# Latent attention: both query tiles' score products of a pair of heads issued together

## What is computed

```python
def mla_attend(q_nope, q_rope, k_nope, k_rope, v):
    scale = (MLA_NOPE_DIM + MLA_ROPE_DIM) ** -0.5
    s = (jnp.einsum("bqhd,bkhd->bhqk", q_nope, k_nope)
         + jnp.einsum("bqhr,bkr->bhqk", q_rope, k_rope)).astype(jnp.float32) * scale
    p = jax.nn.softmax(s, axis=-1)
    return jnp.einsum("bhqk,bkhe->bqhe", p.astype(v.dtype), v)
```

## Time and profile before

| | us |
|---|---|
| median of three runs | 3077.1 |
| lowest and highest run | 3072.35 and 3080.65 |
| the profiled execution (its span) | 3078.2 |
| busy in it: TensorE, VectorE, ScalarE, GpSimd | 3009.2, 1838.9, 1474.6, 1102.2 |

### The profile page before, as it was taken

One profiled execution on the slowest core, in us unless ns is written; L12 is line 12 of the kernel. 1 busy time (PEld: TensorE's weight loads), 2 busy tenths in 40 slices (PEclk: granted clock), 3 DMA queues, 4 the chain that ended last, 5 costly groups with the idle time before them and its releaser, 6 DMA issues.

```text
span 3078.2 us, 49499 instructions
## 1 busy us (share of the span) xinstructions
PE 3009.2 (98%) x20284; PEld 2627.8 (85%) x20284; DVE 1838.9 (60%) x3263; ACT 1474.6 (48%) x2497; POOL 1102.2 (36%) x428
## 2 busy tenths in 40 slices
PE   7999999999999999999999999999999999999999
PEld 5888887877788886799999877888999978879999
DVE  2777775566675546576465465664465366654654
ACT  3453333454533325565465446654365356654553
POOL 0422222000322231255455423444545423435554
PEclk9999999999999999999999999999999999999999
DMA  7545652211456732278355433334555533335554
GB/s 250 200 153 194 202 191 91 74 56 42 137 202 241 253 115 65 60 258 270 122 165 181 149 110 87 113 104 137 178 161 169 156 98 110 105 115 165 165 191 137
DMA packets 404560, 459.90 MB, mean 149 GB/s; under 512 B 8688, under 2 KB 381424, under 8 KB 404336
## 3 DMA queue, kind: packets, MB, share of 16 engines
q1 hardware_dynamic: 401248, 453.32, 45.7%
q10 hardware_dynamic: 3088, 3.42, 0.3%
HBM read 455.66 MB, written 1.05 MB: 148 GB/s over the span
## 4 chain that ended last, share of the span: by engine, by line
PE 91%; DVE 5%; ACT 2%; issue 1%; DMA 1%; ACTq 0%; POOL 0%; DVEq 0%
PE bank L445 25%; PE bank L447 24%; PE bank L446 24%; PE banks L445 1%; PE banks L447 1%; PE banks L446 1%; PE banks L2585 1%; PE bank L1456 1%; PE bank L649 1%; PE banks L1467 1%; PE banks L2598 1%; DVE wl L405 1%; DMA X<-in_ctxT 1%; PE bank L2546 1%; PE banks L1804 1%
## 5 line engine op out<-in xcount | busy, mean ns | idle before, releaser
L420 POOL TENSOR_TENSOR wl<-raw,wh 128x768 fp32r<-128x768 f32 (+3 forms) x324 | 980.2, 3026 | 1812.8 <-ACT wh L386 1812.8
L386 ACT ACTIVATE wh<-raw 128x2048 fp32r<-128x2048 f32 (+1 forms) x336 | 636.1, 1893 | 458.6 <-PE bank L447 395.9
L405 DVE TENSOR_TENSOR wl<-raw,wh 128x1280 fp32r<-128x1280 f32 (+3 forms) x332 | 495.3, 1492 | 450.1 <-ACT wh L386 449.9
L445 PE MATMUL bank<-nh,wh 128*128 128x272 f32 (+1 forms) x1712 | 506.8, 296 | 3.4 <-DVE nl L2168 2.8
L447 PE MATMUL bank<-nh,wl 128*128 128x272 f32 (+1 forms) x1712 | 494.8, 289 | 0.0
L446 PE MATMUL bank<-nl,wh 128*128 128x272 f32 (+1 forms) x1712 | 493.1, 288 | 0.0
L445 PE MATMUL bank<-xh,wh 128*128 128x512 f32 (+2 forms) x1282 | 441.0, 344 | 4.2 <-DVE xl L783 3.7
L447 PE MATMUL bank<-xh,wl 128*128 128x512 f32 (+2 forms) x1282 | 433.8, 338 | 0.0
L446 PE MATMUL bank<-xl,wh 128*128 128x512 f32 (+2 forms) x1282 | 433.6, 338 | 0.0
L445 PE MATMUL bank<-hh,wh 128*128 128x512 f32 (+1 forms) x1024 | 344.1, 336 | 0.0
L446 PE MATMUL bank<-hl,wh 128*128 128x512 f32 (+1 forms) x1024 | 344.1, 336 | 0.0
(11 more groups left out here) (470 smaller groups left out, 5614.5 us busy)
## 6 DMA issues: line engine op xcount, KB each, us to landing
raw<-in_mlp_w SPq DMA_DIRECT2D x128, 1024.0 KB, 5.6
raw<-in_w_in SPq DMA_DIRECT2D x60, 1024.0 KB, 5.2
raw<-in_mod_wT SPq DMA_DIRECT2D x48, 1024.0 KB, 5.0
extra<-in_mod_wT SPq DMA_DIRECT2D x36, 1024.0 KB, 5.4
raw<-in_w_mlp_up SPq DMA_DIRECT2D x32, 1024.0 KB, 5.4
raw<-in_w_mlp_down SPq DMA_DIRECT2D x32, 1024.0 KB, 5.1
raw<-in_w_in SPq DMA_DIRECT2D x34, 512.0 KB, 5.0
raw<-in_w_ssd_down SPq DMA_DIRECT2D x16, 1024.0 KB, 5.1
```

Source lines behind the costliest of these rows:

```text
L386: nc.scalar.activation(self.wtile(self.wh, c1), self.rawtile(c1), AF.Copy).then_inc(*up("act_wh", ("wh", c1)))
L405: nc.vector.tensor_tensor(l, r, h.bitcast(F32), ALU.subtract).then_inc(*up("dve_wl", ("wl_dve", c1), *([("wl_pool", c1)] if n == self.P[c1 ...
L420: nc.gpsimd.tensor_tensor(l, r, h.bitcast(F32), ALU.subtract).then_inc(*up("pool_wl", ("wl_pool", c1), *([] if n else [("wl_dve", c1)])))
L445: nc.tensor.matmul(o, ah, bh, start=first, stop=False)
```

## The change

The score products of both query tiles of a pair of heads are issued together: the four content products, and then the four rope products. They are followed by the transposes and the value products of two older units in turn. Only TensorE's list changes, and in it only the order and the places of some waits: `pe_bank` is now called directly in front of each content product, so that the wait for each of the four banks stands between the products. ScalarE's, VectorE's, GpSimd's and SyncE's lists are the same as before.

```diff
-        for s in range(19):
-            self.pe_mla_step(s)
-            if s in (16, 17):
-                self.pe_mwo(s - 16, 0, 6)
+        for s in range(0, 20, 2):
+            if s < 16:
+                self.pe_mla_scores(s)
+            for u in (s - 2, s - 1):
+                if 0 <= u < 16:
+                    self.pe_mla_turn(u)
+                if 0 <= u - 1 < 16:
+                    self.pe_mla_values(u - 1)
+                if s >= 16 and u < 16:
+                    self.pe_mwo(u - 14, 0, 6)
...
+    def pe_mla_scores(self, s0):
...
         nc, at, up, PE = self.nc, self.T.at, self.T.up, self.PE
...
+        p = s0 // 2
+        PE.wait_ge(*at("mqn", p))
+        PE.wait_ge(*at("mkn", p))
+        PE.wait_ge(*at("turned", "m", p // 2))
+        PE.wait_ge(*at("mkturned"))
+        PE.wait_ge(*at("mkcopied"))
+        for q in range(2):
+            for i in range(2):
+                b = self.pe_bank((2 * q + i,), "ms", s0 + q, i)
                 r = slice(64 * i, 64 * i + 64)
-                nc.tensor.matmul(b[:], self.mQN[r, p, qs], self.mKN[r, p, :], start=True, stop=False)
-            for i, b in enumerate(bs):
+                nc.tensor.matmul(b[:], self.mQN[r, p, 128 * q:128 * q + 128], self.mKN[r, p, :], start=True, stop=False)
+        for q in range(2):
+            for i in range(2):
                 r = slice(32 * ((2 * p + i) % 4), 32 * ((2 * p + i) % 4) + 32)
-                nc.tensor.matmul(b[:], self.mQR[r, p // 2, qs], self.mKR[r, :], start=False, stop=True).then_inc(*up("pe_scores", ("acc", "ms", s, i)))
...
+                nc.tensor.matmul(self.place["ms", s0 + q, i][:], self.mQR[r, p // 2, 128 * q:128 * q + 128], self.mKR[r, :], start=False, stop=True
+                                 ).then_inc(*up("pe_scores", ("acc", "ms", s0 + q, i)))
```

More of the change, by code:

```diff
@@ L1768, in pe_mla_query @@
             self.pe_rope(("m", n // 2), self.mQR[:, n // 2, :], 256, self.permm[:], (7,))
-    def pe_mla_step(self, s):
+    def pe_mla_scores(self, s0):
         nc, at, up, PE = self.nc, self.T.at, self.T.up, self.PE
[L1772 to L1780, removed]
-            for i, b in enumerate(bs):
+        p = s0 // 2
[7 more added lines that the diff above has]
+                b = self.pe_bank((2 * q + i,), "ms", s0 + q, i)
@@ L1787, in pe_mla_step @@
-        u = s - 2
-        if 0 <= u < 16:
-            for i in range(2):
[L1790 to L1806, removed]
+                nc.tensor.matmul(self.place["ms", s0 + q, i][:], self.mQR[r, p // 2, 128 * q:128 * q + 128], self.mKR[r, :], start=False, stop=True
+                                 ).then_inc(*up("pe_scores", ("acc", "ms", s0 + q, i)))
@@ new lines, in pe_mla_turn, with pe_mla_values @@
+    def pe_mla_turn(self, u):
+        nc, at, up, PE = self.nc, self.T.at, self.T.up, self.PE
+        for i in range(2):
+            b = self.pe_bank((4 + i,), "mt", u, i)
+            PE.wait_ge(*at("mp", u, i))
+            for t in range(4):
+                ins = nc.tensor.transpose(b[:, 128 * t:128 * t + 128], self.mE[u % 3][:, i, 128 * t:128 * t + 128], self.ident[:])
+            ins.then_inc(*up("pe_turned", ("acc", "mt", u, i)))
+    def pe_mla_values(self, u):
+        nc, at, up, PE = self.nc, self.T.at, self.T.up, self.PE
+        p, q = u // 2, u % 2
+        b = self.place["mo", p] if q else self.pe_bank((6 + p % 2,), "mo", p)
+        PE.wait_ge(*at("mv", p // 4, 3))
+        for i in range(2):
+            PE.wait_ge(*at("mpt", u, i))
+        for t in range(4):
+            for i in range(2):
+                ins = nc.tensor.matmul(b[64 * i:64 * i + 64, 128 * q:128 * q + 128], self.mV[:, t, 128 * p + 64 * i:128 * p + 64 * i + 64],
+                                       self.mPT[u % 2][:, 4 * i + t, :], start=(t == 0), stop=(t == 3))
+        ins.then_inc(*up("pe_values", ("acc", "mo", u)))
```

## The result

| | before | after |
|---|---|---|
| median, us (11 runs each, side by side) | 3077.41 | 3085.30 |
| lowest and highest | 3072.35, 3081.66 | 3080.20, 3088.03 |
| profiled execution (span) | 3078.2 | 3084.4 |

The ratio is 1.0027, with a 95% interval of 1.0018 to 1.0036. That is 8.3 us slower (5.5 to 11.1): clearly slower, but by less than the 0.3% (9.2 us) that was called no change, with the upper end of the interval beyond it. The forecast was 3085.5.

What follows compares the result with a forecast made beforehand. TensorE bounds the kernel now; after the change a loop through three engines would pace the latent attention. 7.4 us late plus 1.2 for the clock, 8.6 on the median 3077.1, gives 3085.7, rounded 3085.5; range 3079 to 3093.

Steps and rivals of the forecast that it cites:

- What the change saves: TensorE in the latent attention: sixteen merges of score groups at 0.20 us each take off 3.2 us.
- The start: Start of the latent attention: first transposes (unit 0) at 1222.3 against 1217.52, late by 4.8 us.
- The two stops: TensorE standing still at the stage's start, about 2 us twice within 5.5 us, from 1214.0 and from 1217.4.
- The pairs: Steady state of the latent attention: 8.85 us per pair of units, 0.52 more than now.
- The last step: End of the pair's cycle: 1.59 us from the odd unit's exponentials until TensorE may write the next odd unit's content products.
- the loop: Cycle through TensorE, ScalarE and VectorE that sets a pair's time: 8.85 us, above the 7.93 TensorE needs.
- The sum: Latent attention stage: 7.4 us late at unit 14's transposes, plus 1.2 for the clock, in all 8.6 us.
- The fall of the clock: Groups before the first transposes run partly at half rate after the stops: 0 to 1.8 us, taken as 1.2.
- (a): TensorE stays the bound after the start: a pair takes 7.93 us, +1.2 us in all, 3078; chance 0.12.
- (b): Clock falls again and again at a 0.9 us stop in every pair: 4 to 10 us, 3090 to 3096; chance 0.14.
- (c): Merged group doesn't run through, so 0.20 us isn't saved: loop 9.05, 1.6 us more, 3087; chance 0.05.
- (d): Nothing waits in the latent attention and the 3.2 us are gained: 3073.9; chance 0.03.

Runs made afterwards that it cites:

- e1: Changed kernel, but TensorE waits for all four banks before the first of the four content products; ratio to the kernel before 1.0055 (1.0039 to 1.0071).
- e6: Changed kernel with first four units in old order, then per pair content even, rope even, rope odd, content odd; ratio to before 0.9992 (0.9983 to 1.0000).
- e4: Changed kernel plus filler products on TensorE at the start, three before unit 2's content products, one before unit 3's; ratio to before 1.0024 (1.0013 to 1.0036).
- e2: Changed kernel with units still paired but unmerged, in the order content, rope, content, rope; ratio to the kernel before 1.0008 (0.9999 to 1.0017).
- e5: Changed kernel with ScalarE's copy of the transposes put behind the two exponentials instead of ahead of them; one run, 3088.64 us.
- e7: Score order content even, rope even, rope odd, content odd, after an old-order start, plus transposes, values, values, transposes; ratio to before 0.9989 (0.9980 to 0.9999).
- e3: Changed kernel with the first four units in the order of before, merged pairs from unit 4 on; ratio to the kernel before 1.0012 (1.0004 to 1.0021).

## Why the prediction was right, and where by luck

**What the change saves: right.** 1.92 us for a rope group, as worked out from the windowed attention, and 1.92 for a content group that nothing holds up (e1). By that count TensorE has 3.2 us less to do, and e6 collects a part of such a saving where nothing is in its way: 0.20 us a pair. The rule of the Trainium skill (TensorEngine Tiling (Array Packing), Key Properties), that a change of the tiling mode makes TensorE drain, is borne out for the scores by these 0.20 us. For values between transposes the same merge brought 0.08 us, less than half of it.

**The start: right in its mechanism.** With the clock undisturbed (e4) the first transposes come 12.14 us behind the first product, forecast 12.2. The two stops were forecast at 2 us each and came out at 1.53 and 0.33. Each head's content product waits for its own exponential, so that head 0's starts 0.83 us behind the first exponential (1247.12 to 1247.95) where the forecast had both heads start 1.59 behind it; and at half rate unit 2's products fill most of the second stop.

**The pairs: right, and 0.13 us too long.** 8.72 where the sum said 8.85. The last step was put at 1.59, from exponentials to a content group that began anew; for head 1's product, the later of the two, it is 1.50 inside a running group (the odd unit's exponentials start at 1247.12, head 1's product at 1248.62). And from maxima to exponentials it is 1.50 (1254.33 to 1255.83) when both banks are ready, not 1.53. That e1 lengthens a pair by 0.96, e2 removes the stop and e5 moves it is the evidence for the loop.

**The sum: two terms mis-sized in opposite ways, and a total that was met by luck.** Without the clock the stage loses 6.5 us (e4), forecast 7.4; six pairs at 0.13 less are 0.8 of the difference. The fall of the clock costs 3.2 us, forecast 1.2 within 0 to 1.8: that term was mis-sized, since the clock stayed down not for the 3 us up to the first transposes but for 13. The two errors, -0.9 and +2.0, cancel in part only. The stage loses 9.7 us where 8.6 were forecast: unit 14's transposes start at 1282.49 against 1272.76. That the median of 3085.3 lies 0.2 us from the forecast is luck, as single runs of one kernel lie up to 9 us apart.

In the profiled executions the span grew by 6.2 only. The other 3.5 us are given back after the stage, where the prediction took nothing back. Windows, of before and of after at the same work:

```profile
1840.00:1960.00 120.00, 117.86 (x907) 95.03 (x906) 75.79 (x205) 75.09 (x208) 40.31 (x14) 0.99 0.33 94
...
2480.00:2540.00 60.00, 56.26 (x373) 45.60 (x372) 44.62 (x104) 32.84 (x83) 11.77 (x5) 0.91 0.29 91
```

```profile
1850.00:1970.00 120.00, 117.86 (x916) 95.78 (x915) 77.21 (x209) 77.01 (x209) 40.43 (x15) 1.00 0.34 99
...
2486.00:2546.00 60.00, 54.95 (x385) 44.84 (x384) 45.67 (x107) 34.35 (x85) 11.79 (x5) 0.97 0.30 95
```

The instructions of these stretches are the same in both kernels. The clock fell at short stops of the second block in the one execution and not in the other, and each such place moves the later stages by about 1.5 us: the shift of the same instruction goes from 9.7 us behind the stage to 9.3 at 1850, then from 9.3 to 7.9 between 1890 and 1930, from 7.9 to 6.5 near 2100, from 6.6 to 5.1 between 2480 and 2540, and back from 5.1 to 6.2 near 2780. An example: in the kernel before TensorE stands still for 1.29 us up to 1901.58, and the granted clock from 1902 to 1905.2 is 0.50; in the changed kernel it is 1.00 at the same place (1912 to 1915). In the profiled execution of e4 next to nothing was given back or added: its instructions are 8.2 us late behind the stage (6.5 from the stage, 1.7 from a later start of it) and 8.3 at the end (3086.5 against 3078.2). So a single execution carries several us of this, as the runs of the kernel before do (3072 to 3082), and 3 us in the stage can't be seen in six runs. The +8.3 us over 11 runs, with an interval of 5.5 to 11.1 that holds the 9.7 of the stage, fits the mechanism. Whether the missing 1.4 us are chance, or come of the later start of all that follows, is open.

**The rivals.** (a) didn't come: the loop is 8.72, over 8.33. (b) neither: the clock is 1.00 behind 1229. (c) neither: the rope groups run through in 1.92 us. (d) neither: the stage is 9.7 us longer; e6 and e7 collect a part of that gain by another order.

## What to carry to other kernels

Before products are grouped to save changes of shape, follow one unit through all engines and back to the bank that it frees: what counts is not TensorE's own time but what comes to stand behind the product that waits. Keep the half of a pair that is ready complete before the half that waits (e6), and build up a pipeline's first units one at a time (e3). A gain of 0.1% is shown by the stage's own distances in the trace; the time of the whole kernel moves by 0.3% from one execution to the next (3072 to 3082 us).

## What was not expected of the hardware

* Behind a stop of 1.53 us at the start of the stage the granted clock was 0.50 for 13 us on end, while TensorE was busy for 12.67 of them; no stretch shown of the kernel before is that long (7 us in the earlier trace rows), and e4, with the stops filled, shows 1.00 there. In e1 a stop of 5.36 us cost only one content group at half speed. The length of a stop doesn't tell how long the clock stays down, nor whether it falls at all; what does isn't settled.
* Two products of one group that lie in different halves of the rows of the array start each when its own bank is free: head 0's product of the odd unit starts at 1247.95, head 1's at 1248.62, while two whose banks are free show as one row (x4 or x8) with a common start.
* The price of a change of shape isn't one number: merging saves 0.20 us between content and rope products (8.33 to 8.13 us a pair, e6), and 0.08 where two value groups merge between transposes (e7).
